# Router logits taken from the unnormed rows, and the last tile of the output projection gated in halves

## The reference, cut to what matters

```python
    # mixed: 2048 x 1024, convolution heads and HGRN heads side by side
    x = x + g1 * einsum('bnc,cd->bnd', mixed, w_out)                  # output projection, gated residual
    h = rmsnorm(x, norm2_g) * (1 + sc2) + sh2                         # norm 2, modulated
    logits = einsum('bnd,de->bne', h, router)                         # 16 logits a token
    probs = softmax(logits, axis=-1)
    gate, idx = top_k(probs.transpose(0, 2, 1), 256)                  # each expert takes 256 tokens
    # then SwiGLU of each expert on its rows of h, times gate, added into x at idx, times g2
```

## Time and profile before

| | |
|---|---|
| time, median of 3 runs (lowest, highest) | 2253.72 us (2253.41, 2254.76) |
| profiled execution: time, span | 2256.41 us, 2254.7 us |
| TensorE busy over the span | 2133.5 us (95%), 14453 matmuls |
| VectorE, ScalarE, GpSimd busy | 1554.8 us (69%), 977.4 us (43%), 437.0 us (19%) |
| output projection stage | from about 964 us to about 1163 us of the span |
| counting and lists (`topk_stage`) | from about 1163 us to about 1204 us |
| first products of the experts | from about 1219 us to the end |

### The profile page before, as it was taken

How to read it: one execution, slowest core, us unless ns; L and a number is a source line. 1 busy time by engine, 2 the same in 40 slices (tenths; PEclk the granted TensorE clock), 3 DMA queues, 4 the chain that set the end, 5 groups by cost and what they waited for, 6 DMA issues and landing times. The chain is left out here.

```text
span 2254.7 us, 37689 instructions
## 1 busy us (share of the span) xinstructions
PE 2133.5 (95%) x14453; PEld 1416.5 (63%) x14453; DVE 1554.8 (69%) x2194; ACT 977.4 (43%) x1343; POOL 437.0 (19%) x448
## 2 busy tenths in 40 slices
PE   6799999999999999999976999999999999999995
PEld 3344444444778787745524777777777777777772
DVE  2849999785667786765566667666666666766666
ACT  4511002355566556545542444443444444443444
POOL 1510001011446565300012111101111011101111
PEclk8899999999999999899977999999999999999998
DMA  9341002444110311375454887777877878777786
GB/s 354 100 76 33 20 17 87 130 151 145 34 52 15 87 45 38 120 258 178 159 194 141 267 257 248 238 247 241 270 245 240 263 243 265 240 240 251 252 265 266
DMA packets 280296, 392.92 MB, mean 174 GB/s; under 512 B 101507, under 2 KB 142979, under 8 KB 279693
## 3 DMA queue, kind: packets, MB, share of 16 engines
q1 hardware_dynamic: 261770, 333.10, 45.2%
q0 software_dynamic: 16528, 56.47, 9.0%
q10 hardware_dynamic: 1908, 2.18, 0.3%
HBM read 313.44 MB, written 62.54 MB: 167 GB/s over the span
## 5 line engine op out<-in xcount | busy, mean ns | idle before, releaser
L91 PE MATMUL pgu<-xhi,mwlo 128*128 128x256 bf16 x2048 | 558.7, 273 | 0.0
L90 PE MATMUL pgu<-xlo,mwhi 128*128 128x256 bf16 x2048 | 558.7, 273 | 0.0
L89 PE MATMUL pgu<-xhi,mwhi 128*128 128x256 bf16 x2048 | 558.7, 273 | 0.0
L2493 DVE TENSOR_TENSOR mwlo<-mwst,mwhi 128x2048 bf16<-128x2048 f32 x187 | 427.1, 2284 | 0.0
L2393 ACT ACTIVATE mwhi<-mwst 128x2048 bf16<-128x2048 f32 x186 | 350.8, 1902 | 9.7 <-DMA mwst<-in_w_gate 9.6
L2401 ACT ACTIVATE thb<-pgu 128x256 f32<-128x256 f32 x128 | 49.1, 383 | 544.6 <-PE pgu L91 544.6
L708 DVE SCALAR_TENSOR_TENSOR co<-u,taps,co 128x1984 f32<-128x1984 f32 (+22 forms) x120 | 234.2, 1951 | 3.7
L2504 DVE SCALAR_TENSOR_TENSOR thb<-thb,pgu 128x256 f32<-128x256 f32 x128 | 53.9, 421 | 244.9 <-ACT thb L2401 244.9
L89 PEld LDWEIGHTS pgu<-xhi,mwhi 128*128 128x128 bf16 x2048 | 200.4, 98 | 24.9
L90 PEld LDWEIGHTS pgu<-xlo,mwhi 128*128 128x128 bf16 x2048 | 200.4, 98 | 24.7
L91 PEld LDWEIGHTS pgu<-xhi,mwlo 128*128 128x128 bf16 x2048 | 200.4, 98 | 23.0
(11 more groups left out here) (395 smaller groups left out, 4090.1 us busy)
## 6 DMA issues: line engine op xcount, KB each, us to landing
mwst<-in_w_gate SPq DMA_DIRECT2D x32, 2048.0 KB, 9.1
mwst<-in_w_up SPq DMA_DIRECT2D x32, 2048.0 KB, 8.0
mwst<-in_w_down SPq DMA_DIRECT2D x32, 2048.0 KB, 11.8
wst<-in_w_in SPq DMA_DIRECT2D x28, 512.0 KB, 6.1
big<-in_ada_w SPq DMA_DIRECT2D x5, 2048.0 KB, 19.0
s_rows<-row SPq DMA_DIRECT2D x16, 520.0 KB, 5.6
u<-in_ada_w SPq DMA_DIRECT2D x8, 1024.0 KB, 6.2
xt<-in_x SPq DMA_DIRECT2D x16, 512.0 KB, 4.4
```

The lines of the kernel that those rows point to most:

```text
L89: nc.tensor.matmul(out, lh, rh, start=(first and k == 0), stop=False)
L90: nc.tensor.matmul(out, lh, rl, start=False, stop=False)
L91: ins = nc.tensor.matmul(out, ll, rh, start=False, stop=(last and k == n - 1))
L2493: nc.vector.tensor_tensor(wlo[:, b, ks], wst[:, b % NS, ks], whi[:, b, ks], ALU.subtract)\
```

## The change

The transposes take `x1` where they took `h2`, so a tile can be turned before it is normed. The router weights are scaled once by A (`rwA = rw * A`, A being formed in columns, `mcol`), and the shift's part of the logits, sh2 @ router, is formed once by eight matmuls (`shift_products`, 16 columns each, with sh2 spread over a 128x128 block in `shb`) and kept in `crow`. VectorE then makes `lgs = plg * r + crow` ahead of the largest logit. The columns of sc2, sh2 and norm2_g come by three new transfers on ScalarE's queue, each of 1024 single numbers. `h2` is still formed, for the stored rows. In `last`, tile 15 is gated in two halves, its routing stands ahead of its row's cast and low half, the routing of tiles 13 and 14 stands ahead of tile 15's second half, and the turn and logits of tiles 13 and 14 stand between the projection's products. `EARLY` goes from 4 to 2. `route` is split: the copy of the probabilities into the stored row is `share`.

The diff, cut to its core:

```diff
@@ -1648,7 +1648,7 @@
     NCK = P // NE
...
     STEPS = 15
-    EARLY = 4
+    EARLY = 2
...
         self.g_ps = m.sem("g_ps")
@@ -1704,6 +1704,11 @@
         m = Mem(nc, ctx)
...
         rw = m.sb("rw", [P, KD, CH])
+        rwA = m.sb("rwA", [P, KD, CH])
+        mcol = m.sb("mcol", [P, 4, KD])
+        shb = m.sb("shb", [P, KD, P])
+        crow = m.sb("crow", [P, NE])
+        lgs = m.sb("lgs", [P, 2, NE])
         pick = m.sb("pick", [P, NE])
...
         mrow = m.sb("mrow", [P, 3, D])
@@ -1815,6 +1824,11 @@
                                   .partition_broadcast(P)).then_inc(s_in if j else g_in, 16)
...
                 act.dma_start(rw[:, :, 0:NE], I["router_w"][0].rearrange("(k p) e -> p k e", p=P)).then_inc(rw_in, 16)
+                with nc.allow_non_contiguous_dma(reason="three rows of 1024 numbers into columns"):
+                    for j, r in enumerate((2, 1)):
+                        act.dma_start(mcol[:, j], scr["modrows"][2 * r:2 * r + 2, :].rearrange("a n -> (a n)")
+                                      .rearrange("(k p) -> p k", p=P)).then_inc(mc_in, 16)
+                    act.dma_start(mcol[:, 2], I["norm2_g"][0].rearrange("(k p) -> p k", p=P)).then_inc(mc_in, 16)
...
                     wait(act, x1_ok[p], n + 1)
@@ -1839,7 +1853,7 @@
...
                     wait(act, mx_ok[p], n + 1)
-                    nc.scalar.activation(pe_[:, p], plg[p], ACT.Exp, bias=nm[:, p, 0:1], accum_out=nm[:, p, 1:2])\
+                    nc.scalar.activation(pe_[:, p], lgs[:, p], ACT.Exp, bias=nm[:, p, 0:1], accum_out=nm[:, p, 1:2])\
                         .then_inc(ex_ok[p], 1)
...
                 def step(t, p, n, have):
@@ -1852,19 +1866,31 @@
                     if have[0]:
...
+                def front_halves(p, n):
+                    wait(act, hx_ok, 1)
+                    nc.scalar.activation(junk[:, FH[0]], x1[:, p, FH[0]], ACT.Square, accum_out=st[:, p, 3:4]).then_inc(hs_ok, 1)
+                    wait(act, x1_ok[p], n + 1)
+                    nc.scalar.activation(junk[:, FH[1]], x1[:, p, FH[1]], ACT.Square, accum_out=st[:, p, 0:1])\
+                        .then_inc(ss_ok[p], 1)
+                    wait(act, ss_ok[p], n + 1)
+                    wait(act, hb_ok, 1)
+                    nc.scalar.activation(st[:, p, 1:2], st[:, p, 0:1], ACT.Sqrt, bias=st[:, p, 3:4], scale=1.0 / D)\
+                        .then_inc(sd_ok[p], 1)
+
                 def last(engine, n):
...
                     cast(0, n)
-                    front(NT - 1, 1, n)
                     turn(0, n)
+                    partial(0, n)
                     route(1, n - 1)
-                    partial(0, n)
+                    route(0, n)
+                    front_halves(1, n)
                     turn(1, n)
-                    route(0, n)
+                    nc.scalar.preload_act_table(ACT.Exp)
                     partial(1, n)
+                    route(1, n)
                     cast(1, n)
-                    route(1, n)
...
@@ -1883,10 +1909,24 @@
                     wait(dve, s_in, 48)
...
                     wait(dve, sc_ok, 1)
+                    wait(dve, mc_in, 48)
+                    nc.vector.scalar_tensor_tensor(mcol[:, 3], mcol[:, 0], 1.0, mcol[:, 2], ALU.add, ALU.mult).then_inc(mc_ok, 1)
+                    nc.vector.tensor_copy(shb[:], mcol[:, 1].unsqueeze(2).broadcast_to([P, KD, P])).then_inc(mc_ok, 1)
+                    wait(dve, mc_ok, 2)
+                    wait(dve, rw_in, 16)
+                    wait(dve, rz_ok, 1)
+                    nc.vector.tensor_tensor(rwA[:], rw[:], mcol[:, 3].unsqueeze(2).broadcast_to([P, KD, CH]), ALU.mult)\
+                        .then_inc(mc_ok, 1)
+
+                def shift_logits():
+                    wait(dve, cr_ps, 1)
+                    nc.vector.tensor_copy(crow[:], pcr).then_inc(cr_ok, 1)
+                    wait(dve, cr_ok, 1)
...
                     wait(dve, x1_ok[p], n)
+                    wait(dve, tp_ps[p], n)
                     nc.vector.tensor_tensor(t1[:, p], pout[p][:].rearrange("p a j -> p (a j)"), mrow[:, 0], ALU.mult)\
...
                     wait(dve, x_in[p], n * 16 + 16)
@@ -1900,7 +1940,7 @@
                     nc.vector.reciprocal(st[:, p, 2:3], st[:, p, 1:2]).then_inc(rs_ok[p], 1)
...
                     wait(dve, x1_ok[p], n + 1)
-                    wait(dve, tp_ps[p], n)
+                    wait(dve, hi_ok[p], n)
                     nc.vector.scalar_tensor_tensor(h2[:, p], x1[:, p], st[:, p, 2:3], mrow[:, 1], ALU.mult, ALU.mult)\
...
                     wait(dve, hn_ok[p], n + 1)
@@ -1912,12 +1952,18 @@
...
                     wait(dve, lg_ps[p], n + 1)
-                    nc.vector.tensor_reduce(nm[:, p, 0:1], plg[p], AX.X, ALU.max, negate=True).then_inc(mx_ok[p], 1)
+                    wait(dve, rs_ok[p], n + 1)
+                    wait(dve, ex_ok[p], n)
+                    nc.vector.scalar_tensor_tensor(lgs[:, p], plg[p], st[:, p, 2:3], crow[:], ALU.mult, ALU.add).then_inc(ls_ok[p], 1)
+                    wait(dve, ls_ok[p], n + 1)
+                    nc.vector.tensor_reduce(nm[:, p, 0:1], lgs[:, p], AX.X, ALU.max, negate=True).then_inc(mx_ok[p], 1)
                     wait(dve, ex_ok[p], n + 1)
...
                         .then_inc(zp_ok, 1)
+
+                def share(p, n):
                     nc.vector.tensor_scalar(prob[:, p, :], pe_[:, p], nm[:, p, 2:3], None, ALU.mult)\
...
@@ -1926,21 +1972,46 @@
                         gated(t, p, n)
...
                         scales()
+                    if isinstance(t, int) and t == 1:
+                        shift_logits()
                     if have[2]:
                         route(t - 2, p, n - 1)
+                        share(p, n - 1)
                     if have[1]:
...
+                def gated_half(c, p, n):
+                    if c == 0:
+                        wait(dve, half_ps, 1)
+                        wait(dve, x1_ok[p], n)
+                        wait(dve, tp_ps[p], n)
+                    else:
+                        wait(dve, out_ps[p], n + 1)
+                    nc.vector.tensor_tensor(t1[:, p, FH[c]], pout[p][:, c, :], mrow[:, 0, FH[c]], ALU.mult).then_inc(t1_ok[p], 1)
+                    if c == 0:
+                        wait(dve, x_in[p], n * 16 + 16)
+                        wait(dve, x1_out[p], n * 16)
+                        wait(dve, ss_ok[p], n)
+                    wait(dve, t1_ok[p], n + 1 + c)
+                    nc.vector.tensor_tensor(x1[:, p, FH[c]], xt[:, p, FH[c]], t1[:, p, FH[c]], ALU.add)\
+                        .then_inc(x1_ok[p] if c else hx_ok, 1)
+
                 def last(engine, n):
                     low(0, n)
-                    gated(NT - 1, 1, n)
+                    gated_half(0, 1, n)
+                    route(NT - 3, 1, n - 1)
+                    share(1, n - 1)
+                    route(NT - 2, 0, n)
+                    wait(dve, hs_ok, 1)
+                    nc.vector.tensor_scalar(st[:, 1, 3:4], st[:, 1, 3:4], 1.0 / D, EPS, ALU.mult, ALU.add).then_inc(hb_ok, 1)
+                    gated_half(1, 1, n)
+                    share(0, n)
                     front(NT - 1, 1, n)
-                    route(NT - 3, 1, n - 1)
-                    route(NT - 2, 0, n)
+                    route(NT - 1, 1, n)
                     low(1, n)
-                    route(NT - 1, 1, n)
+                    share(1, n)
...
                 wait(dve, pt_ps, 1)
@@ -1948,6 +2019,14 @@
...
             def _(pe):
+                def shift_products():
+                    wait(pe, rw_in, 16)
+                    wait(pe, mc_ok, 3)
+                    for k in range(KD):
+                        last = nc.tensor.matmul(pcr, shb[:, k, :], rw[:, k, 0:NE], start=(k == 0), stop=(k == KD - 1),
+                                                skip_group_check=True)
+                    last.then_inc(cr_ps, 1)
+
                 def project(t, p, n, c, ks=slice(0, KD)):
...
                     mine = K["last_mx"][:, :, bass.ds(t * P, P)]
@@ -1965,24 +2044,25 @@
                         last = out_products(nc, K, p, c, slice(4, KD) if start else ks, mine)
...
                         last.then_inc(out_ps[p], 1)
+                    if c == 0 and isinstance(t, int) and t == NT - 1:
+                        last.then_inc(half_ps, 1)
                 def turn(p, n):
-                    wait(pe, h2_ok[p], n + 1)
+                    wait(pe, x1_ok[p], n + 1)
                     wait(pe, tp_ok[1 - p], n + p)
                     for k in range(KD):
-                        last = nc.tensor.transpose(ptp[:, k // 4, (k % 4) * P:(k % 4 + 1) * P], h2[:, p, k * P:(k + 1) * P],
+                        last = nc.tensor.transpose(ptp[:, k // 4, (k % 4) * P:(k % 4 + 1) * P], x1[:, p, k * P:(k + 1) * P],
                                                    K["ident"][:])
...
                     if isinstance(n, int) and n == 0:
-                        wait(pe, rw_in, 16)
```

(27 more changed lines are left out.)

## The result

| | before | of the change |
|---|---|---|
| time, median (lowest, highest) | 2254.24 us (2253.41, 2256.33), 4 runs | 2270.5 us (2270.25, 2274.02), 4 runs |
| ratio, 95% interval | | 1.0072 (1.0061 to 1.0084) |
| profiled execution: time, span | 2256.41, 2254.7 us | 2274.02, 2272.3 us |

The change costs 16.3 us. The forecast was 2266.6, +12.9 against its base, with slower at 0.93: the sign and the mechanism came as forecast, and the size is 3.9 us larger.

What follows compares the result with a forecast made beforehand. TensorE was taken to bound the output projection, with an engine chain at its end. Head +13.0, loop 0, end -0.1 and `EARLY` 0 gave +12.9 us on the 2253.7 median: 2266.6, range 2260.5 to 2272.5.

Steps and rivals of the forecast that it cites:

- TensorE's stand: Between tiles 0 and 1, TensorE idles from about 972.7 to 981.7 waiting for VectorE's new instructions: 9.0 us.
- shift products at full clock: On TensorE ahead of tile 1, the eight shift products show as 16 rows and take 2.04 us.
- loss to the clock: Behind TensorE's stand, 3.3 to 4.6 us at half clock lose 1.65 to 2.3 us, taken as 2.0.
- head of the stage: Start of the output projection: stand, shift products and clock loss together 13.0 us, between 8.3 and 17.8.
- loop: Projection tiles: VectorE's added instruction, about 0.2 us a tile, is covered by projection products; taken as 0.
- end, to the copy into `pr`: Tile 15's end: Z 1.1 us earlier but VectorE's last copy about level; -0.1 us, between -1.1 and +1.5.
- landing of `mcol`: Column transfers behind `rw` on ScalarE's queue: 3072 numbers take 3.3 to 3.6 us, landed at about 979.9.
- lower bound of the forecast: Head of the stage: columns landed by 977.57, when VectorE has formed A in rows; stand 6.2 us.
- rival B: Head of the stage: single numbers share engines with loads of x and mixed rows; +17.8 us, 2271.5; chance 0.13.
- Rival C: Stage's end: a 1.3 us pause behind each ScalarE table load; 2267.9 to 2269.2; chance 0.08.
- D: Stage's end saves 3.9 us and shift products cost only their 2.0: 2251.8; chance 0.03.
- E: No difference: the stand is absorbed by TensorE's waits further on; 2253.7; chance 0.04.

Runs made afterwards that it cites:

- e1: The change with the shift products moved into tile 2's step and the `crow` copy to the end of tile 1's step: 2264.1 us, ratio 1.0040 to before.
- e4: The change with `EARLY` back to 4: 2271.6 us, ratio 1.0077 to the kernel before.
- e2: The change with its three column transfers issued on GpSimd's queue in place of ScalarE's: 2266.4 us, ratio 1.0054 to the kernel before.
- e10: e5 with the columns loaded as 24 rows of 128 and transposed once on TensorE: 2255.8 us, ratio 1.0002 to the kernel before.
- e11: e10 with the shift summed on VectorE and one product in place of eight: 2256.4 us, ratio 1.0007 to the kernel before.
- e3: The change plus 48 unused products on TensorE ahead of its wait for the shift products: 2268.8 us, ratio 1.0064 to the kernel before.
- e8: The kernel of the change, run again unaltered: 2271.6 us, ratio 1.0078 to the kernel before.
- e6: e5 with the three column transfers also moved to GpSimd's queue: 2258.5 us, ratio 1.0018 to the kernel before.
- e5: e1 with VectorE's three column instructions behind tile 0's front and the `crow` copy back behind tile 1's gate: 2260.6 us, ratio 1.0030 to before.
- e9: The kernel before with only the three column transfers added on ScalarE's queue, their data unused: 2255.1 us, ratio 1.0000 to before.

## Why the prediction was right in kind and 3.9 us short

| step | forecast | measured | |
|---|---|---|---|
| TensorE's stand | 9.0 | 11.0 | 971.64, where the next product was due, to 982.62 |
| shift products at full clock | 2.04 | 1.7 | e1, until the next product |
| loss to the clock | 2.0 | 4.6 | 1.7 in the products, 2.9 in tile 1 |
| head of the stage | 13.0 | 17.3 | tile 2's gate from the stage's first operation: 43.0 against 25.7 |
| loop | 0 | -0.3 | 144.6 against 144.9 |
| end, to the copy into `pr` | -0.1 | -0.4 | |
| copy to counting | - | +0.2 | 1.74 against 1.51 |
| EARLY | 0 | 0 | e4 |
| sum | 12.9 | 16.8 | medians +16.3 |

**The stand.** The mechanism holds: VectorE at the columns, TensorE at `rwA`, all of the projection behind it. The mis-sized term is the landing of `mcol`, forecast 15.7 us into the stage (979.9) and measured at 18.0 (981.24, VectorE's start). The forecast took the transfers to be issued one right behind the other behind `rw` and counted the time of their numbers, 3.3 to 3.6 us. At its best the rate was as forecast (921 packets of this queue between 978 and 979 us), in the two microseconds behind it 513 and 579. But the issues of the first two transfers of 1024 single numbers held the queue 4.5 us each, and most of the numbers of the last two moved only from 978 on. The row that I took for such an issue, `taps`, was on GpSimd's queue, where it took 1.75 us for 3968 numbers; I read its landing and not whose queue it was on. In e2, with the issue out of the way, the columns had landed by about 972.4 (the last was issued at 964.62, and the slowest took 7.8 us to land), and the last broadcast, which came 1.2 us later into the stage than before, decided: near the lower bound of the forecast. From the landing to TensorE's start VectorE's three instructions took 1.4 us and not 1.8, since the spread is a copy of 0.69 us. The time is near rival B's, 2271.5, but B's cause, engines shared with the loads of x and mixed rows, is at most a part: the queue of these loads took 68% of the engines in the microsecond of 921 packets, and 2% in the one of 579. So that the range held the time is in part luck: its upper end stood on B's cause.

The Trainium skill says ("DMA: Bandwidth & Descriptors", section Rules for kernel authors) that a non-contiguous last dimension becomes one descriptor for each element and should be rearranged. The traces agree in their packets: between 962 and 985 us this queue moved 1616 before, 4736 in the change and 1664 in e10, with whole rows and a transpose. ScalarE's queue is held 3.5 us for all three transfers in e10 against 9.7 in the change; in e11, with the same transfers as e10, 4.4.

**The products.** The 2.04 us were taken from the earlier trace rows as if at full clock; the window from 936.7 to 940.7 us had a granted clock of 0.88 on the mean, and scaled by that the row gives 1.8 (an estimate), near the 1.86 of e1.

**The clock.** That a stand brings 0.50 was right (rows above), and e3 shows that it costs. The length was mis-sized: the earlier trace rows had 3.3 and 4.6 us behind stands of 2.8 and 7.0; here it was 8.9 behind 11.0. In that stretch lie the 3.4 us of narrow shift products and 5.5 us of projection at half speed. Two rows of the trace were too few for a range: the same head had 8.3 us at half clock in e8 and 7.5 in e4, and e2 had 8.0 behind a stand of 7.3. The loss of 4.6 us is that of the one profile; in e8 and e4 it was 4.2 and 3.7.

**The end.** x1 later by 3.3 (3.4 forecast), Z earlier by 1.4 (1.1), the last copy bound by cast, `low` and share, as forecast. TensorE waits 0.43 and 0.78 us for tile 13's and 14's turn, 1.2 together; the forecast had 1.2 at tile 14's alone. Rival C falls: Sqrt starts at 1170.82 behind a load from 1169.52 for 1.28, the `lgT` copy at 1173.33 behind one from 1172.04, and the turn's copy ahead of that load ends at 1172.02. By the Trainium skill's rule on the drain ("ScalarE: Activation LUTs", section What ACT_TABLE_LOAD costs) about 1.38 us would lie beside each load; this trace does not show them. D and E fall with the stand. D's idea, that the end would win 3.9 us if the head were free, is answered by e6: against the kernel before it wins 0.4.

## What to carry to other kernels

A new product of a bound engine is priced by when its operand is ready and by what stands behind it in the queue, not by its own 1.9 us: placed some 12 us later, behind work that was there anyway, and with its loads in whole rows, it costs +0.8 (e10; the interval includes 0, and the stage is 1.6 longer) where it cost +16.3. Move the work that prepares the operand too, and mind where the copy of the result stands: in e1 both still made TensorE wait. And read the issue row of a transfer, not only its landing: load columns as whole rows and turn them.

## What the runs showed of the hardware

- On ScalarE's queue two transfers of 1024 single numbers held the engine 4.5 us each in the change (7.6 to 9.6 us for the two in e1, e3, e4, e5, e8 and e9), and a third behind them 0.6. Why the third is short, and so what holds the issue, is open. Issued by GpSimd (e2) they took 0.9 each. As eight rows of 128 the two took 3.2 us together in e10, 4.0 in e11.
- On ScalarE's queue the 3072 numbers went as packets of their own (4736 of this queue between 962 and 985 us against 1616 before). On GpSimd's (e2) the same three transfers show as 96 packets in all.
- The half clock lasted 8.9 us behind a stand of 11.0, though TensorE was busy without a break from 982.62 to 991.00. In e1, behind a stand of 3.75 us, the clock was still 1.00 when TensorE resumed at 991.30, and fell to 0.50 only at about 992.5. What decides its length is open.
- A table load of ScalarE costs 1.28 us and no more: with loads at 1169.52 and 1172.04 the instructions around them follow within 0.02 us.
